# Sparse attention by query: value products in head pairs with stationary values, and normalisation moved ahead of them

## The reference, cut to what matters

```python
p_cmp = jnp.where(jnp.any(ok_c, axis=-1)[:, None], jax.nn.softmax(sc, axis=-1), 0.0)
o_cmp = jnp.einsum('bgrqc,bcgd->bqgrd', p_cmp.astype(dt), cv)          # 31 compressed keys
...
p_slc = jax.nn.softmax(ss.reshape(b, g_, r_, NSA_QBLOCK, -1), axis=-1).reshape(ss.shape)
o_slc = jnp.einsum('bgrqnl,bgqnld->bqgrd', p_slc.astype(dt), vg)       # selected blocks
...
p_win = jax.nn.softmax(sw, axis=-1)
o_win = jnp.einsum('bgrqk,bkgd->bqgrd', p_win.astype(dt), vwb)         # window
o = gb[..., 0:1] * o_cmp + gb[..., 1:2] * o_slc + gb[..., 2:3] * o_win
```

## Time and profile before

| what | value |
|---|---|
| time of three runs | 4073.93, 4076.91, 4080.45 us; median 4076.91 us |
| profiled execution | 4073.59 us, of it span 4071.6 us |
| PE busy | 3707.0 us (91%) |
| PEld, DVE, ACT busy | 2826.8 us (69%), 1605.0 us (39%), 1202.9 us (30%) |
| sparse attention, first product to last | 1283.1 to 1504.7 us |

### The profile page before, as it was taken

One profiled execution on the slowest core, in us unless ns is written; L12 is line 12 of the kernel. 1 busy time (PEld: TensorE's weight loads), 2 busy tenths in 40 slices (PEclk: granted clock), 3 DMA queues, 4 the chain that ended last, 5 costly groups with the idle time before them and its releaser, 6 DMA issues. The chain is left out here.

```text
span 4071.6 us, 44570 instructions
## 1 busy us (share of the span) xinstructions
PE 3707.0 (91%) x17898; PEld 2826.8 (69%) x17898; DVE 1605.0 (39%) x2538; ACT 1202.9 (30%) x2003; POOL 168.8 (4%) x282
## 2 busy tenths in 40 slices
PE   7879798999999999989996999799999888888999
PEld 5448677778666887778775854488887745666777
DVE  5343334433402343343334533344433435534443
ACT  3122223222213443332233120322222435533222
POOL 0033010000000001010000000000000011000000
PEclk9879899999999999999998989899999999998999
DMA  3326231222311002122221201111112300011212
GB/s 137 143 105 228 114 124 63 81 85 101 120 42 42 1 11 110 56 83 103 83 103 48 92 0 42 42 42 64 65 57 93 137 21 21 1 42 62 82 72 103
DMA packets 30051, 307.72 MB, mean 76 GB/s; under 512 B 3843, under 2 KB 5604, under 8 KB 9157
## 3 DMA queue, kind: packets, MB, share of 16 engines
q1 hardware_dynamic: 29894, 305.52, 20.1%
HBM read 303.41 MB, written 2.10 MB: 75 GB/s over the span
## 5 line engine op out<-in xcount | busy, mean ns | idle before, releaser
L561 PE MATMUL psum<-operand_rounded,weights_rest 128*128 128x512 f32 (+1 forms) x1360 | 522.1, 384 | 61.9 <-DVE operand_rest L532 61.9
L562 PE MATMUL psum<-operand_rounded,weights_rounded 128*128 128x512 f32 (+1 forms) x1360 | 518.8, 381 | 0.0
L563 PE MATMUL psum<-operand_rest,weights_rounded 128*128 128x512 f32 (+1 forms) x1360 | 518.1, 381 | 0.0
L530 DVE TENSOR_TENSOR weights_rest<-ring,weights_rounded 128x1024 fp32r<-128x1024 f32 x170 | 208.2, 1224 | 578.0 <-ACT operand_rounded L513 578.0
L326 PE MATMUL psum<-operand_rounded,weights_rest 128*128 128x512 f32 (+1 forms) x1056 | 380.1, 360 | 53.1 <-DVE weights_rest L345 53.1
L327 PE MATMUL psum<-operand_rounded,weights_rounded 128*128 128x512 f32 (+1 forms) x1056 | 378.4, 358 | 0.0
L512 ACT ACTIVATE weights_rounded<-ring 128x1024 fp32r<-128x1024 f32 x170 | 179.9, 1058 | 631.8 <-PE psum L563 557.9
L561 PEld LDWEIGHTS psum<-operand_rounded,weights_rest 128*128 128x128 f32 x1360 | 261.7, 192 | 114.5 <-issue 55.1
L562 PEld LDWEIGHTS psum<-operand_rounded,weights_rounded 128*128 128x128 f32 x1360 | 262.0, 193 | 47.5
L563 PEld LDWEIGHTS psum<-operand_rest,weights_rounded 128*128 128x128 f32 x1360 | 261.3, 192 | 48.1
L326 PEld LDWEIGHTS psum<-operand_rounded,weights_rest 128*128 128x128 f32 x1056 | 200.9, 190 | 89.8 <-issue 59.9
(11 more groups left out here) (437 smaller groups left out, 6224.3 us busy)
## 6 DMA issues: line engine op xcount, KB each, us to landing
ring<-in_ff_w SPq DMA_DIRECT2D x32, 2048.0 KB, 7.5
ring<-in_w_mod SPq DMA_DIRECT2D x24, 2048.0 KB, 7.6
ring<-in_ffn_up SPq DMA_DIRECT2D x22, 2048.0 KB, 7.5
ring<-in_ffn_down SPq DMA_DIRECT2D x33, 1024.0 KB, 4.8
ring<-in_a_w_in SPq DMA_DIRECT2D x4, 2048.0 KB, 11.2
ring<-in_xa_wk SPq DMA_DIRECT2D x4, 2048.0 KB, 7.4
ring<-in_xa_wv SPq DMA_DIRECT2D x4, 2048.0 KB, 7.5
ring<-in_xa_wq SPq DMA_DIRECT2D x4, 2048.0 KB, 7.5
```

Of the source, the lines that this page charges most:

```text
L530: dve.tensor_tensor(parts["weights_rest"][:, r % 2, :], weight_rows(s, r), parts["weights_rounded"][:, r % 2, :].bitcast(F32), ALU.subtrac ...
L561: nc.tensor.matmul(k.bank(m, n), rest, top_in, start=first, stop=False)
L562: nc.tensor.matmul(k.bank(m, n), top, top_in, start=False, stop=False)
L563: mm = nc.tensor.matmul(k.bank(m, n), top, rest_in, start=False, stop=last)
```

## The change

`sparse_attention` takes the place of `attention_by_query`, and `heads_by_feature` goes:

- The mask is no longer a PE product. DVE adds the causal tile to the diagonal block of both branches in PSUM (one instruction), then reduces.
- The exponentials also write their sums (`accum_out`). DVE takes the inverse, multiplies by the gate, and scales both branches of `probs` in SBUF; `turn` waits for that.
- The values are the stationary operand (64 columns) and the transposed probabilities the moving one. Two heads, the units u - 1 and u, go together in even steps: one writes PSUM partitions 0 to 63, the other 64 to 127 of the same bank; the compressed branch and both branches accumulate there. `turned` has three buffers in place of two.
- DVE copies the pair's bank to `k.h`, which is already by feature.

```diff
-def attention_by_query(k, units, branches, score_matmuls, width_of, value_rhs, vw, gates, out, arena, extra=None):
+def sparse_attention(k, units, scores, width_of, values, compressed, gates, out, masked, arena):
...
             def turn(u):
-                pe.wait_ge(*p_ready.at(B * (u + 1)))
-                for i, part in enumerate(parts[u]):
-                    n = before[u] + i
+                pe.wait_ge(*p_norm.at(u + 1))
+                for b in range(B):
+                    n = B * u + b
                     if n >= 2:
 
                         pe.wait_ge(*t_copied.at(n - 1))
...
+            def head_products(u):
+                rows = slice(64 * (u % 2), 64 * (u % 2) + 64)
+                blocks = width_of(u) // P
+                listed = [(rows,) + compressed(u) + (True, False)]
                 for b in range(B):
                     for kb in range(blocks):
-                        at = b * (BANK if B > 1 else 0) + kb * P
-                        mm = nc.tensor.matmul(into[:, b * (vw + 1):(b + 1) * (vw + 1)], turned[:, u % 2, at:at + P], value_rhs(u, b, kb),
-                                              start=(kb == 0), stop=(kb == blocks - 1))
+                        at = b * BANK + kb * P
+                        listed.append((rows, values(u, b, kb), turned[:, u % held, at:at + P], False, b == B - 1 and kb == blocks - 1))
+                return listed
+
+            def pair_values(u):
+                pe.wait_ge(*t_copied.at(B * (u + 1)))
+                if u >= 5:
+                    pe.wait_ge(*o_taken.at((u - 5) // 2 + 1))
+                for two in zip(head_products(u - 1), head_products(u)):
+                    for rows, lhs, rhs, first, last in two:
+                        mm = nc.tensor.matmul(out_bank(u)[rows, :], lhs, rhs, start=first, stop=last)
                 mm.then_inc(o_ready.sem, 1)
...
-                if step >= 3:
-                    values(step - 3)
+                if step >= 3 and step % 2 == 0:
+                    pair_values(step - 3)
...
-                    nc.scalar.activation(probs[:, u % 3, to:to + n], k.psum[:, base:base + n], ACT.Exp,
-                                         bias=small[:, u % 4, b:b + 1]).then_inc(p_ready.sem, 1)
+                    nc.scalar.activation(probs[:, u % 3, to:to + n], k.psum[:, base:base + n], ACT.Exp, bias=small[:, u % 4, 0, b:b + 1],
+                                         accum_out=small[:, u % 4, 1, b:b + 1]).then_inc(p_ready.sem, 1)
...
+                if masked:
+                    block = score_tiles(u, n)[:, :, n - P:n]
+                    nc.vector.tensor_tensor(block, block, masked, ALU.add).then_inc(s_masked.sem, 1)
+                    dve.wait_ge(*s_masked.at(u + 1))
+                nc.vector.tensor_reduce(small[:, u % 4, 0, :], score_tiles(u, n), AX_X, ALU.max, negate=True).then_inc(s_max.sem, 1)
+
+            def normalise(u):
+                n = width_of(u)
+                dve.wait_ge(*p_ready.at(B * (u + 1)))
+                nc.vector.reciprocal(small[:, u % 4, 2, :], small[:, u % 4, 1, :]).then_inc(p_step.sem, 1)
+                dve.wait_ge(*p_step.at(2 * u + 1))
+                nc.vector.tensor_tensor(small[:, u % 4, 3, :], small[:, u % 4, 2, :], gates(u), ALU.mult).then_inc(p_step.sem, 1)
+                dve.wait_ge(*p_step.at(2 * u + 2))
+                for b in range(B):
+                    part = probs[:, u % 3, b * BANK:b * BANK + n]
+                    op = nc.vector.tensor_scalar(part, part, small[:, u % 4, 3, b:b + 1], None, ALU.mult)
+                op.then_inc(p_norm.sem, 1)
+
+            def copy_pair(u):
+                dve.wait_ge(*o_ready.at(u // 2 + 1))
+                nc.vector.tensor_copy(out(u), out_bank(u)).then_inc(o_taken.sem, 1)
 
-            for step in range(U + 4):
+            for step in range(U + 5):
                 if step < U:
                     maximum(step)
-                if step >= 4 and step % 2 == 1:
-                    take_pair(step - 4)
+                if 1 <= step <= U:
+                    normalise(step - 1)
+                if step >= 5 and step % 2 == 0:
+                    copy_pair(step - 5)
...
-    attention_by_query(k, units, 2, scores, lambda u: (units[u][0] + 1) * P, values, NSA_DIM, two_gates, pair_out, 23592, extra=compressed)
-    heads_by_feature(k, O)
-    ident_scope.close()
+    sparse_attention(k, units, scores, lambda u: (units[u][0] + 1) * P, values, compressed, two_gates, pair_out, both_branches, 23592)
     output_product(k, norm=following, memory=True)
```

More of the change, by code:

```diff
@@ L957, in attention, with score_tiles, out_bank @@
     o_copied.base += heads
-def attention_by_query(k, units, branches, score_matmuls, width_of, value_rhs, vw, gates, out, arena, extra=None):
+def sparse_attention(k, units, scores, width_of, values, compressed, gates, out, masked, arena):
     nc = k.nc
-    U = len(units)
-    B = branches
-    wide = B * BANK if B > 1 else max(width_of(u) for u in range(U))
+    U, B, held = len(units), 2, 3
+    wide = B * BANK
     probs = k.region(arena, 3, wide)
[L970 to L990, removed]
+    turned = k.region(arena + 3 * wide, held, wide)
+    small = k.region(arena + (3 + held) * wide, 4, 4, B)
+    s_ready, s_max, p_ready, p_step, p_norm = (k.counter(n) for n in ("query_scores", "query_max", "query_exponentials", "query_weights", "query_normed"))
+    t_ready, t_copied, o_ready, o_taken = (k.counter(n) for n in ("query_turned", "query_turned_copied", "query_heads", "query_heads_taken"))
+    s_masked = k.counter("query_masked")
     def score_bank(u, b):
         return (2 * (u % 2) + b) * BANK
-    def out_slot(u):
-        at = (6 + (u // 2) % 2) * BANK + (u % 2) * slot
-        return k.psum[:, at:at + slot]
+    def score_tiles(u, n):
+        base = score_bank(u, 0)
+        return k.psum[:, base:base + wide].rearrange("p (b n) -> p b n", b=B)[:, :, 0:n]
+    def out_bank(u):
+        return k.bank(6 + (u // 2) % 2, P)
     with nc.Block() as block:
@@ L1012, in score @@
                     base = score_bank(u, b)
-                    for cols, lhs, rhs, first, last in score_matmuls(u, b):
+                    for cols, lhs, rhs, first, last in scores(u, b):
                         mm = nc.tensor.matmul(k.psum[:, base + cols.start:base + cols.stop], lhs, rhs, start=first, stop=last)
@@ L1017, in turn @@
             def turn(u):
[L1018 to L1020 removed]
+                pe.wait_ge(*p_norm.at(u + 1))
+                for b in range(B):
+                    n = B * u + b
                     if n >= 2:
                         pe.wait_ge(*t_copied.at(n - 1))
[L1024 to L1025 removed]
+                    for at in range(0, width_of(u), P):
+                        mm = nc.tensor.transpose(k.bank(4 + n % 2)[:, at:at + P], probs[:, u % 3, b * BANK + at:b * BANK + at + P], k.c("ident"))
@@ L1086, in maximum @@
                 dve.wait_ge(*s_ready.at(u + 1))
[L1087 to L1094, removed]
-                nc.vector.tensor_reduce(small[:, u % 4, 0:B], src, AX_X, ALU.max, negate=True).then_inc(s_max.sem, 1)
@@ L1135, in attention_by_query @@
+    for s in (s_ready, s_max, p_norm) + ((s_masked,) if masked else ()):
         s.base += U
     p_ready.base += B * U
-    t_ready.base += before[-1]
-    t_copied.base += before[-1]
+    p_step.base += 2 * U
+    t_ready.base += B * U
+    t_copied.base += B * U
+    o_ready.base += U // 2
     o_taken.base += U // 2
-    o_step.base += 3 * (U // 2)
-def heads_by_feature(k, O):
-    nc = k.nc
-    made = k.counter("heads_flipped")
-    with nc.Block() as block:
-        @block.sync
-        def _(sp):
-            k.prefetch(sp)
-        @block.tensor
-        def _(pe):
-            for m in range(KT):
-                for t in range(TT):
-                    mm = nc.tensor.transpose(k.bank(m)[:, t * P:(t + 1) * P], O[:, t, m * P:(m + 1) * P], k.c("ident"))
-                mm.then_inc(made.sem, 1)
-        @block.scalar
-        def _(act):
-            for m in range(0, KT, 2):
-                act.wait_ge(*made.at(KT))
-                nc.scalar.activation(k.h[:, m, 0:SEQ], k.bank(m), ACT.Copy)
-        @block.vector
-        def _(dve):
-            for m in range(1, KT, 2):
-                dve.wait_ge(*made.at(KT))
-                nc.vector.tensor_copy(k.h[:, m, 0:SEQ], k.bank(m))
-    made.base += KT
```

79 lines of the change are left out of this document (16 added, 63 removed).

## The result

The changed kernel takes 4094.2 us (median of five runs, 4092.1 to 4097.4), 1.0041 times the kernel before, 95% interval 1.003 to 1.0053. I had said 4063, with 4053 to 4075 for the range: the time moved the other way. The profiled execution has a span of 4090.3 us where it was 4071.6, 18.7 more. From the first score of the sparse attention to ACT's first rounding for the output product (L512) it was 231.6 us (1283.11 to 1514.69) and is 248.6 (1284.63 to 1533.18): 17.0 us. The stage begins 1.5 us later; behind it the distance stays the same.

What follows compares the result with a forecast made beforehand. PE bounds the stage before; after the change, a chain of waits through DVE and ACT. Stage 4.6 us, its tail 0.95 and heads_by_feature 8.2, less 0.5, gain 13 us: 4063 us, range 4053 to 4075.

Steps and rivals of the forecast that it cites:

- the latent attention: Another stage used as model for the changed one: same shape, PE held up in each pair of steps, clock 1.00.
- rival 4: Sparse attention: clock stays at half through the tiles of 2 and 1 blocks, 27 us lost, total 4090; 5%.
- rival 3: Sparse attention: clock falls for short stretches at 2 and 1 blocks, costing 3 to 8 us, total 4066 to 4071; 16%.
- The mask's products: PE's mask work behind the scores: 0.29 us a unit, saved on PE when DVE adds the mask.
- The chain: Linked waits from score to next score in sparse attention: 9.2, 7.5, 5.8, 4.15 us per pair at 4 to 1 blocks.
- the wait that ends PE's idle time: Before the transposes of every second step, PE stands until ACT's copy L1063 is done.
- its successor: If ACT's copy weren't late, DVE's normalisation L1091 would be the next to end PE's wait before the transposes.
- PE's own sum: PE's work per pair of units at k blocks: 1.73k + 0.67, so 7.6 us at 4 and 2.4 at 1.
- rival 1: Sparse attention: PE stays the bound, or DVE alone limits; stage 180 us, total 4025; 7%.
- The end: Behind the stage: one copy replaces take_pair's five DVE instructions and heads_by_feature goes, gaining 0.95 and 8.2 us.
- The shape per half: Compressed pair within the value products: a shape change paid per interleaved half would cost 0.15 us more for 32 pairs, 5 us.
- rival 5: Value products: the two halves don't run together, so values double, 42 us more, total 4105; 3%.

Runs made afterwards that it cites:

- e1: Changed kernel with spare products of 384 columns, read by nobody, ahead of the transposes in every second step: 4062.9 us, 0.9972 of the kernel before.
- e5: Kernel before with only the causal mask moved, added by DVE in place of the two PE products: 4083.7 us, 1.0019 of the kernel before.
- e4: Changed kernel with the mask added by PE again, none on DVE: 4048.1 us, 0.9927 of the kernel before.
- e11: Changed kernel with four spare transposes of the identity ahead of the scores of every second step: 4067.2 us, 0.9978 of the kernel before.
- e2: Changed kernel with ACT copying the turned probabilities before it does the exponentials: 4051.6 us, 0.994 of the kernel before.
- e3: Changed kernel with ACT's copies before its exponentials and, in odd steps, DVE's normalisation before its maximum: 4026.8 us, 0.9881 of the kernel before.
- e9: Changed kernel with four spare products of rounded identity and rounded mask ahead of the scores of every second step: 4068.8 us, 0.9979 of the kernel before.
- e10: Changed kernel with two spare transposes of the identity ahead of the scores of every second step: 4087.4 us, 1.0021 of the kernel before.

## Why the prediction was wrong

- **The step that failed**: the sum was made at the full clock throughout, that is, it put the cost of half clock at nothing. The ground was the latent attention, with the same shape and 1.00; and rival 4 got only 5% because "PE never idles over 1.8 us in a pair, and work at half clock fills the gaps". The term left out measured 29.6 us: 248.6 us of stage in the changed kernel, 218.9 in e1, which does more work and has the same pairs at full clock.
- **Both halves of that ground were true, and protected nothing.** After the first pairs no wait of PE in the stage was longer than 1.7 us. At half clock the work does fill the gaps (16.89 of 17.10 us busy from 1446.3), and the clock stayed at half.
- **The latent attention is no proof**, though it isn't far off: 183.93 of 212.5 us busy (0.87), with waits of 0.79 us in a pair. The changed kernel at 4 blocks and full clock, just before a fall, has 0.85, with waits of 1.25:
```profile
1296.10:1320.00 23.90, 20.34 (x141) 12.43 (x140) 15.73 (x35) 13.81 (x35) 0.00 (x0) 1.00 0.00 1
```
- **A slip in rival 3**: "57 to 65%" of the time for PE at 1 and 2 blocks doesn't follow from the prediction's own sums. At 2 blocks they give 4.13 of 5.8 us, 71%.
- **The mask's products**, 0.29 us of PE work a unit, were counted as a pure saving on PE. Taking them out of the kernel before, by itself, loses the clock in the tile of 1 block (e5); putting them back into the changed kernel holds it nearly throughout (e4); and other work of nearly that size holds most of it (e11). e4 also shows that the rest of the change, with the mask left on PE, costs hardly any clock: 7.7 us at half.
- **Rival 4** is what happened, and more: half clock at 1 block and in part at 2, and short stretches at 4 and 3. Its price per pair was low: 8 x 1.2 forecast at 1 block, 1.49 a pair measured; 2.15 at 2 blocks, 2.5 measured (8.29 in the pair from 1446.66, less 5.75). The price doubled the products alone; if the changes of shape, 0.45 a pair, double as well, it is 1.6 and 2.6. That its 4090 came within 4 us of 4094.2 is in part luck: it had all of the 2-block tile at half clock, where some 27 of 57 us were, and nothing at 4 and 3 blocks, where there were 24 us. Its condition, about half of the last 80 us at half clock, was met by 17 + 60 us.
- **The chain** was right: 9.2, 7.5, 5.8, 4.15 forecast, 9.08, 7.41, 5.74, 4.08 measured at full clock. So was the wait that ends PE's idle time (L1063), its successor (L1091, by e2), and PE's own sum (e3). e3 comes to rival 1's 4025 (4026.8), but only with the orders of ACT and DVE turned, so this doesn't speak for rival 1.
- **The end**: 9.15 us forecast, 10.0 to 0.85 measured. Right.
- **The shape per half** (the rule weighed there) costs nothing more: from the values' start to the next score are 2.27 us at 4 blocks (1341.78 to 1344.05), where 0.436k + 0.22 and the two changes of shape behind the entering one, 0.30, give 2.26. The halves run together (rival 5 falls).

**What stays open.** Why e5's clock falls with PE busy 11.34 of 12 us, and e4's is held with 19.65 of 24, isn't settled. The runs show that spare work of either kind holds the clock, and that more transposes hold it longer (0, 0.22, 0.44 us a pair: 104, 91, 26 us at half). They don't show what the chip counts, and time on PE alone doesn't order the runs: e9, with 0.48 us a pair, has 41.6 us at half, more than e11 with 0.44; and e4, which has the same four rounded products in a pair as e9, but behind the scores and without the mask add on DVE, has 7.7. What of this is place, what is the shorter pair, and what is scatter between executions, no run separates. The 6.8 us near 1289, where the first pairs have little overlap, stayed in every variant of the changed kernel and of e5, but not in e4.

## What to carry to other kernels

Work that is taken off TensorE can take its clock along, as it did here: before a stage is thinned out on TensorE, price it at both clock levels, and look whether the sum still gains at half clock. If it doesn't, shorten the chain (here two orders of issue, 67 us from 4094.2 to 4026.8, the regained clock among them), so that PE is the bound again, and only then fill what is left. A busy share next to a clock below 1.00 is no measure of load, since the slower clock makes the same work look busier.

## What the runs showed that I had not expected

- Spare work of 0.22 us in a pair of 4 to 9 us moves the kernel by 20 us (e10 and e11). e10's times scatter from 4078.3 to 4092.4 over ten runs, where most kernels here stay within 8 us.
- The half clock lasts: 68.2 us in one stretch, through the last tile, the barrier and eleven products of the output product; it was full again from 1541.8, with PE at work without a gap since 1536.76.
- Useless work paid: 31 us of the changed kernel's 4094 by products whose result nobody reads.
